# Two transformer blocks on one core: a norm applied as gate-up tiles leave PSUM, Gelu, borders and mixer orders rearranged

## What is computed

```
x = x + post_norm(mixer_2(pre_norm(x)))        # gated delta rule and dilated attention
h = pre_ffn_norm(x)                            # h = x * gain * rstd, rstd per token
u = causal_dwconv(h @ ffn_up, 3 taps) + bias
x = x + post_norm((gelu(gate of u) * val of u) @ ffn_down)
```

## Time and profile before

| | us |
|---|---|
| median of 3 runs | 2065.92 |
| lowest and highest | 2065.55, 2076.42 |
| the profiled execution, its own time | 2066.17 |
| its span, first to last instruction | 2064.3 |
| TensorE busy in it | 1919.4 |
| VectorE, ScalarE, GpSimd busy | 1223.1, 996.8, 652.8 |
| mean granted clock of TensorE | 0.964 |

### The profile page before, as it was taken

The page is one execution under the profiler, slowest core; times in us unless marked ns, Lnnn a source line. Parts: engine busy times, 40 slices in busy tenths (PEclk is TensorE's granted clock), DMA queues, the critical chain, the costliest instruction groups (busy, mean ns, idle before and its releaser), DMA issues.

```text
span 2064.3 us, 41181 instructions
## 1 busy us (share of the span) xinstructions
PE 1919.4 (93%) x15758; PEld 1870.1 (91%) x15758; DVE 1223.1 (59%) x1478; ACT 996.8 (48%) x1304; POOL 652.8 (32%) x595
## 2 busy tenths in 40 slices
PE   6999999999999999999999989879999889779997
PEld 6999999999989999999999989769889789679897
DVE  4655586666456456866664674446664664356655
ACT  5434456544444345564444563445544564445543
POOL 4751301276137513012662016122330025032220
PEclk9999999999999999999999899989999799889999
DMA  6646444465455464444555422114445222124444
GB/s 221 209 164 210 154 144 145 162 206 193 164 195 201 157 215 164 144 146 159 206 190 168 154 102 100 42 64 144 175 144 199 90 102 87 37 82 163 166 164 159
DMA packets 49222, 314.39 MB, mean 152 GB/s; under 512 B 5713, under 2 KB 6865, under 8 KB 19921
## 3 DMA queue, kind: packets, MB, share of 16 engines
q1 hardware_dynamic: 48960, 311.09, 43.7%
q10 hardware_dynamic: 144, 1.69, 0.2%
HBM read 311.71 MB, written 1.05 MB: 152 GB/s over the span
## 4 chain that ended last, share of the span: by engine, by line
PE 62%; DVE 10%; issue 9%; ACT 9%; DMA 5%; POOL 2%; ACTq 1%; DVEq 0%; SPq 0%; POOLq 0%
PE ps L541 15%; PE ps L543 15%; PE ps L542 15%; DMA raw<-in_down_dram 4%; ACT w_hi L1109 4%; DVE w_lo L1567 4%; PE ps L858 3%; PE ps L546 3%; PE ps L547 3%; PE ps L548 3%; DVE conv L1886 2%; ACT conv L1160 2%; PE ps L691 1%; PE ps L731 1%; DVE v L2084 1%
## 5 line engine op out<-in xcount | busy, mean ns | idle before, releaser
L1567 DVE TENSOR_TENSOR w_lo<-raw,w_hi 128x2048 fp32r<-128x2048 f32 (+1 forms) x322 | 713.0, 2215 | 423.6 <-ACT w_hi L1109 423.1
L541 PE MATMUL ps<-xn,w_hi 128*128 128x256 f32 x2688 | 768.5, 286 | 59.6 <-DVE w_lo L1567 14.6
L542 PE MATMUL ps<-xn,w_hi 128*128 128x256 f32 x2688 | 755.7, 281 | 0.0
L543 PE MATMUL ps<-xn,w_lo 128*128 128x256 f32 x2688 | 755.5, 281 | 0.0
L1109 ACT ACTIVATE w_hi<-raw 128x2048 fp32r<-128x2048 f32 (+1 forms) x322 | 562.4, 1748 | 126.5 <-DMA raw<-in_down_dram 83.4
L541 PEld LDWEIGHTS ps<-xn,w_hi 128*128 128x128 f32 x2688 | 516.9, 192 | 74.2 <-issue 44.1
L542 PEld LDWEIGHTS ps<-xn,w_hi 128*128 128x128 f32 x2688 | 515.4, 192 | 0.8 <-issue 0.5
L543 PEld LDWEIGHTS ps<-xn,w_lo 128*128 128x128 f32 x2688 | 515.1, 192 | 0.0
L541 PE MATMUL ps<-h,w_hi 128*128 128x256 f32 x1056 | 294.1, 278 | 4.9 <-DVE w_lo L1567 4.8
L542 PE MATMUL ps<-h,w_hi 128*128 128x256 f32 x1056 | 293.2, 278 | 0.0
L543 PE MATMUL ps<-h,w_lo 128*128 128x256 f32 x1056 | 293.2, 278 | 0.0
(11 more groups left out here) (310 smaller groups left out, 2633.2 us busy)
## 6 DMA issues: line engine op xcount, KB each, us to landing
raw<-in_gu_dram SPq DMA_DIRECT2D x132, 1024.0 KB, 4.9
raw<-in_in_dram SPq DMA_DIRECT2D x70, 1024.0 KB, 4.9
raw<-in_down_dram SPq DMA_DIRECT2D x96, 704.0 KB, 4.1
raw<-in_out_dram SPq DMA_DIRECT2D x16, 1024.0 KB, 4.8
raw<-in_pb_dram SPq DMA_DIRECT2D x4, 1024.0 KB, 4.8
raw<-in_pa_dram SPq DMA_DIRECT2D x4, 1024.0 KB, 4.9
tables_all<-in_tables_dram ACTq DMA_DIRECT2D x1, 1648.0 KB, 7.2
rows<-in_rows_dram SPq DMA_DIRECT2D x2, 768.0 KB, 5.5
```

The costliest lines, as they stand in the source:

```text
L541: pe.matmul(out, w, xh, start=first, stop=False)
L542: pe.matmul(out, w, xl, start=False, stop=False)
L543: return pe.matmul(out, wl, xh, start=False, stop=last)
L1567: dve.tensor_tensor(w_lo[:, r, 0:elems], raw[:, k % RAW_RING, 0:elems], w_hi[:, r, 0:elems], ALU.subtract).then_inc(lo.sem, 1)
```

## The change

1. **Second gate-up.** VectorE multiplies each tile by rstd into conv_in as it leaves PSUM, which frees the pair; all taps read conv_in. ScalarE's order is taps, w_hi of the slot three ahead, Gelu. `v`, its copy and the two forms of low part ahead of the stage go: ScalarE writes xn = x * gain, VectorE its low part, and the sum of squares is made behind the first tile.
2. **Borders.** `rounds` runs body first, then the split; `open_rounds` makes the split of the third slot ahead of the root (ScalarE) or behind the reciprocal (VectorE; in the second block ahead of it). `tile_rounds` takes the place of `rounds` in the down stages. The dummy slots at the end go.
3. **PSUM squares.** ScalarE squares output and down tiles of the second block straight from PSUM and scales them into hm with the gain; TensorE sums the squares chunk by chunk within the stage (`chunk_square`). VectorE takes five chunks of the post norm, GpSimd three.
4. **Mixer orders.** See the lines below. The final norm of the first block goes from VectorE to two wide GpSimd products.
5. **x by another queue.** ScalarE's queue loads x, gains1, ones_d and eps; slot 0 of the weights is split ahead of x.
6. In the first block's output stage the low part of a chunk is written one tile later, and the split comes first.

```diff
-            for c in range(KC):
-                dve.scalar_tensor_tensor(v[:, c], x[:, c], gains2[:, 4 * layer + 2, c:c + 1], rstd[:, 0:T],
-                                         ALU.mult, ALU.mult).then_inc(v_ok.sem, 1)
-                if c >= 2 and c % 2 == 0:
-                    low_even(at, 0, c - 2)
...
             for c in range(KC):
                 x_ready(act, at, 0, c)
+                split_x(c, gains2[:, 4 * layer + 2, c:c + 1])
                 act.activation(sq8[:, c], x[:, c], ACT.Square).then_inc(squared.sem, 1)
...
-                whole = st.name == "gu"
-                if not whole:
-                    for f in range(2):
-                        tile_done(dve, at, st, j, f, g)
-                        dve.tensor_tensor(conv_in[:, j % 2, f], ps[:, 2 * (j % 2) + f, 0:T], rstd[:, 0:T], ALU.mult)\
-                           .then_inc((conv_src, drained)[f].sem, 1)
+                for f in range(2):
+                    tile_done(dve, at, st, j, f, g)
+                    dve.tensor_tensor(conv_in[:, j % 2, f], ps[:, 2 * (j % 2) + f, 0:T], rstd[:, 0:T], ALU.mult)\
+                       .then_inc((conv_src, drained)[f].sem, 1)
...
-                        src = ps[:, 2 * (j % 2) + f, 0:T - s] if whole else conv_in[:, j % 2, f, 0:T - s]
+                        src = conv_in[:, j % 2, f, 0:T - s]
...
+    def rounds(eng, at, st, nxt, count, split, body, behind=None):
         def step(j, g):
             body(j, g)
+            split(at, st.slot0 + j + 1 + LEAD, g, st.elems)
+            if behind:
+                behind(j, g)
...
+    def tile_rounds(eng, at, st, nxt, split, body, steps=cycle):
+        def step(j, g):
+            split(at, st.slot0 + 2 * j + 1 + LEAD, g, st.elems)
+            split(at, st.slot0 + 2 * j + 2 + LEAD, g, st.elems)
+            body(j, g)
+        split(at, st.slot0 + LEAD, 0, st.elems)
+        steps(eng, KC - 2, 2, step)
...
+        def square_out(at, gain, c, src, sq):
+            act.activation(sq[:, c], src, ACT.Square).then_inc(squared.sem, 1)
+            act.activation(hm[:, c], src, ACT.Copy, scale=gains2[:, 4 * at[1] + gain, c:c + 1]).then_inc(x_new.sem, 1)
...
+        def chunk_square(at, n, c, src):
+            pe.wait_ge(squared.sem, squared.upto(at, KC * n + c + 1))
+            ins = pe.matmul(ps[:, AUX, 0:T], ones_d[:], src[:, c], start=c == 0, stop=c == KC - 1)
...
                     if k == 5:
-                        decay_rows_of(1)
+                        query_column()
+                        turn_k()
...
+                if k == 0:
+                    small_product(at, 2 * DN_H, ba_split, ba_hi, ba_lo, SC + 1)
                 if k == 1:
                     rstd_columns(at)
-                    small_product(at, 2 * DN_H, ba_split, ba_hi, ba_lo)
                 if k == 4:
                     decay_rows_of(0)
-                    query_column()
                 if k == 5:
-                    turn_k()
+                    decay_rows_of(1)
...
                 if k == 7:
-                    attend_pv(at, 0, tok[:, V], SC)
                     level_u(LEVELS - 1)
-                    attend_scores(at, 1, 4, SC)
+                    short_scores(at, 2)
+                    short_scores(at, 3)
...
+            attend_out(at, 1, SC)
+            short_turn(at, 3)
+            short_pv(at, 2, tok[:, V])
+            short_pv(at, 3, tok[:, V])
+            head_sums()
+            attend_out(at, 0, SC + 1)
...
+            out_part(0, 0, WC)
+            out_part(1, 0, WC)
+            out_part(2, 0, WC)
+            pe.wait_ge(o_rooted.sem, o_rooted.upto(at, 2))
+            for j in range(3):
+                out_part(j, WC, KC)
+                if j:
+                    chunk_square(at, 0, 2 * j - 2, sq_out)
+                    chunk_square(at, 0, 2 * j - 1, sq_out)
+            out_part(3, 0, KC)
```

More of the change, by code:

```diff
@@ L127 @@
 GROUP = NH // 2
+POOL_ADDS = (1, 4, 7)
+DVE_ADDS = (0, 2, 3, 5, 6)
 RAW_AT = 16 * 1024 + 128
@@ L525, in _ @@
             stream(at, st2["down"], io["down3"])
-        for k in range(LEAD):
-            load((2, DEPTH), k, 0, SLOT, io["in2"][0, k])
         for c in range(KC):
@@ L651, in tile @@
                     last.then_inc(used.sem, 1)
+                    if behind_tile and j and not half:
+                        behind_tile(j - 1)
+            if behind_tile:
+                for j in range(st.pairs):
+                    tile(j, 0)
+                behind_tile(st.pairs - 1)
+                return
             tile(0, 0)
@@ new lines, in _ @@
+            for j in range(3):
[4 more added lines that the diff above has]
+            out_part(3, 0, KC)
+            chunk_square(at, 0, 6, sq_out)
+            chunk_square(at, 0, 7, sq_out)
+            wide(at, st2["gu"], 0, 0, xn, KC, 0, lambda: mean_square_direct(at, 1))
+            wide(at, st2["gu"], 1, 0, xn, KC)
+            with pe.Fori(0, (FC - 2) // 4) as g:
+                for j in range(2, 6):
+                    wide(at, st2["gu"], j, g, xn, KC)
@@ L1496, in _, with short_exp, short_copy @@
                     attend_exp(at, 0)
-                if k == 6:
-                    attend_copy(at, 0, SC)
+            split(at, so.slot0 + 2, 0, SLOT)
             attend_exp(at, 1)
+            act.wait_ge(projected.sem, projected.upto(at, 8))
+            act.activation(four(z_t[:]), four(z_t[:]), ACT.Silu).then_inc(z_ok.sem, 1)
+            act.activation(warm[:, 2:3], eps[:, 0:1], ACT.Exp)
+            def short_exp(u):
+                act.wait_ge(max_ok.sem, max_ok.upto(at, u + 1))
+                for k in range(GROUP):
+                    p = soft[:, 0, k, (u - 2) * P:(u - 1) * P]
+                    act.activation(p, p, ACT.Exp, bias=neg_max[:, u, k:k + 1],
+                                   accum_out=z_sum[:, u, k:k + 1]).then_inc(probs.sem, 1)
+            def short_copy(u):
+                act.wait_ge(pv.sem, pv.upto(at, 2))
+                act.wait_ge(p_turned.sem, p_turned.upto(at, TURNS[u]))
+                copy(p_t[:, u - 2], ps[:, u - 2, :].rearrange("p (k q) -> p k q", k=GROUP)).then_inc(p_out.sem, 1)
             out_copy(1, v_new[:, 0], AUX)
@@ L1838, in _, with low_out @@
             so = st1["out"]
+            def low_out(c):
+                scale_low(at, 1, c, gains1[:, 3 * layer + 2, c:c + 1], xn_lo_odd if c % 2 else xn_lo_even)
             for j in range(4):
+                if j < 3:
+                    split(at, so.slot0 + j + LEAD, 0, SLOT)
                 for f in range(2):
-                    if f == 1 and j < 3:
-                        split(at, so.slot0 + j + LEAD, 0, SLOT)
                     c = 2 * j + f
@@ L2057, in _ @@
[L2057 to L2067 removed]
+            attend_norm(at, 2, 1)
@@ L2091, in post, with add @@
-                scale_next(KC - 2)
-                scale_next(KC - 1)
+                    gain = 4 * layer + 2 if n == 0 else 4 * (layer + 1)
+                    x_ready(dve, at, n, c)
+                    scale_low(at, n, c, gains2[:, gain, c:c + 1], xn_lo_odd if c % 2 else xn_lo_even)
+                follows = k == 1 or layer < DEPTH - 1
+                def add(i):
+                    c = DVE_ADDS[i]
+                    dve.wait_ge(post_dve.sem, post_dve.upto(at, len(DVE_ADDS) * n + i + 1))
+                    dve.tensor_tensor(x[:, c], x[:, c], v[:, c], ALU.add).then_inc(x_dve.sem, 1)
@@ L2094, in _ @@
+                for i, c in enumerate(DVE_ADDS):
+                    dve.tensor_tensor(v[:, c], hm[:, c], rstd[:, 0:T], ALU.mult).then_inc(post_dve.sem, 1)
+                    if i:
+                        add(i - 1)
+                    if follows and i >= 2:
+                        scale_next(i - 2)
+                add(len(DVE_ADDS) - 1)
+                if follows:
+                    for c in range(3, KC):
+                        scale_next(c)
             post(1)
             split(at, so.slot0 + 3 + LEAD, 0, SLOT)
+            open_rounds(at, st2["gu"], split)
```

511 lines of the change are left out of this document (286 added, 225 removed).

## The result

The changed kernel takes 2020.12 us (median of four runs, 2018.53 to 2024.12), against 2065.74 before: 0.977 of the time, 95% interval 0.974 to 0.980. It is faster, by 46 us, where 78 were forecast; 2020 lies above the range, which ended at 2014. The profiled execution took 2018.53 us with a span of 2016.7, so I make the comparison 2064.3 against 2016.7 in spans, 47.6 us.

The account below looks back on a forecast made before the run. TensorE, busy for 93% of the span, was taken as the bound, with time to gain only where it stands or runs at low clock. Terms summed to 78.2 us: 2066.2 to 1988 us, own range 1970 to 2000, full range 1954 to 2014.

Parts of the forecast that it names:

- Gate-up loop: Second block's gate-up: slots fall from 6.06 to 5.6 us (bounds 5.44 and 5.95), 19.2 us gained over two layers.
- The rule that VectorE's taps now contend: Gate-up: taps reading conv_in from SBUF contend with GpSimd; slower rival 8.4 us per slot, 2105 us, chance 0.03.
- Norm ahead of gate-up: Between last output matmul and first gate-up slot's end, norm behind the first tile saves 5.5 us per layer, 11 together.
- Tail: Before the output stage: new mixer orders cut 38.2 us to some 24, 14 per layer; weak-tail rival 2006 us, chance 0.15.
- qkv stage: Second block's qkv: later query column removes waits, 3 us per layer (bounds 0 and 8), plus 1.5 in the first.
- The two new waits that I had named: In qkv: turn_k waits for decay_in(0), and the second decay rows for q2; counted within the 3 us gain per layer.
- two whole-tile GpSimd products at a time when GpSimd is idle: 0: First layer's qkv stage: final scaling of x moves from eight VectorE steps (3.4 us) to GpSimd, at no gain or cost.
- Start: Kernel start: x by another queue and three wide GpSimd sums, first matmul about 12.5 us, 4 us gained (bounds 0 and 7).
- x lands late: Start's lower bound: three MB sharing the engines delay x, so the gain is 0 instead of 4 us.
- Down stages and behind: Second block's down stages and what follows, both layers: PSUM squares and no dummy slots at the end gain 3.5 us together.
- The reciprocal no longer waits for w_lo: Behind the first layer's down stage, where the first matmul waits 12.0 us: this saves 1 to 3 us.
- First block: low_out one tile later gives 6.5 us in output stage and gap behind (bounds 2 and 10), down-stage split order 0.5.

Follow-up runs that it names:

- the one that mends five parts: Changed kernel with the old start, final x and post norms on VectorE, squares behind the last tile, norm ahead of the last split: 2001.93 us.

## Why the prediction failed, and where it held

- **Gate-up loop: right within the stage, with a cost behind it that I left out.** Slots 1 to 21 took 118.7 and 117.5 us where I took 117.6, so 18.9 us came for the 19.2. TensorE's wait for the taps went, as forecast. But the loop of VectorE and ScalarE takes 5.87 us, inside my bounds of 5.44 and 5.95, and TensorE goes faster than that on the slots it has in hand. The sizes came from the qkv stage, where the tap starts after 0.45 us and takes 0.91; here 0.74 and 1.10. What is left over is paid in the second down slot. Of the 22 gate-up stages of the changed kernel and of its edits that leave this loop alone, nine ran at the slow pitch and were followed by a wait of 2.82 to 3.05 us there, thirteen mostly at the fast one, by 4.05 to 4.42: what TensorE gains in the stage it waits for behind it. The rule that VectorE's taps now contend did little harm: one tap of four is held, 1.02 us instead of 0.59, and the four still end with w_hi; w_lo starts first and keeps its 2.29, and GpSimd, which has time, stands.
- **Norm ahead of gate-up: too high.** 3.6 and 2.9 us came for 5.5 each. TensorE starts 7.2 us sooner behind the output stage, but its first slot takes 12.0 and 12.8 us instead of 8.4.
- **Tail: right, mis-sized.** From the same matmul on, 17.4 us in each layer where 14 were taken, and 20.9 left for the estimated 24. The waits for exponents and copies shrank to under 1 us each.
- **qkv stage: wrong in both layers.** "I take 3, twice" failed: from 75.1 and 74.8 us the stretch went to 84.2 and 76.9, a loss of 2.1 us in layer 1, where no GpSimd product stands in it. The two new waits that I had named and thought cheaper than the old ones are its rows: turn_k waits 1.7 us for gam, the second decay rows 2.7 for q. Layer 1 as a whole came out at -16.6 for -17, and that is luck: 5.1 us lost here against 3.4 gained in the tail and 1.3 in the side stage.
- **qkv stage, layer 0: a second step failed**, "two whole-tile GpSimd products at a time when GpSimd is idle: 0". It cost 3.4 to 3.7 us at the same clock; the 6.8 us more at 0.50 in the first profile cost as much again, and in the nine others with this hold the time at 0.50 was anything from 22.2 to 30.7 us. I named the cover on GpSimd's side and did not ask what VectorE does meanwhile, though my own row of 3.79 beside 2.29 was its warning.
- **Start: wrong**, +3.2 for -4. I had counted three wide sums in place of seven as a gain in GpSimd's time, and they hold w_lo and the low parts for 5.3 us; the queue cost 2 us more. The bound "x lands late" was set at 0 gain, where it should have gone below.
- **Down stages and behind: wrong by 16.0 us.** (a) "The reciprocal no longer waits for w_lo": true at the end, where that slot is left out, not in layer 0, where the rows show both copies ahead of it. What is behind the stage went from 12.0 to 12.4 us, where I had -5; taking the squares away from there freed nothing, since the w_lo outlasts them. (b) At the end 16.1 became 13.8, not 11.5: VectorE's products took 0.94, and with all of them on VectorE it is 11.9. (c) In the stream, 5.7 and 8.8 us for the 3.0 of the squares. The rest has three parts. One is the wait in the second down slot, 2.8 and 4.4 us where 2.4 and 1.5 were in all; its w_hi stands behind the last Gelu. The second is the clock, at 0.50 behind that wait, which makes the matmuls there 1.6 and 2.4 us longer. The third is the slow pitch behind the squares, at 4.5 ns a matmul 1.1 and 0.7 us more than before. Together with the 3.0 they make 6.2 and 9.0, slightly too much. I did not look at the last slots of the gate-up stage, where a loop that hides its latency has to pay it.
- **First block:** 12.6 us for the 7. The output stage and the gate-up behind it gave 5.8 for 6.5. The last 3.6 of the rest are one gate-up stage that was slow in the profile of before (127.7) and fast in that of after (124.1), luck and no effect.
- **Range.** The bounds of the terms were added up for the upper end of the gain only; the case that several "nothing" terms cost something at once had no place. The pitch I could have read in the stages of before, 124.2 and 127.7 us for the same work. The three runs of before, whose highest is 10.9 us over the lowest, also said that one execution can move by that much; whether the pitch is all of it is not shown.

## What to carry to other kernels

Work moved to an idle GpSimd is free only if VectorE reads no second SBUF operand meanwhile. If it must be there, cut it into short instructions, or place it so that VectorE's long one starts first. When a loop's latency is hidden inside, price its last iterations too. Read an edit in its own stage before the whole time, since one and the same program spread over 11 us in four executions, and within the stage compare the clock, since half of a difference of 7.2 us was clock here. Begin the stretches before and after at the same instruction: here the tail is 20.9 us from the matmul at which the 38.2 of before begin, and 23.8 from the last side tile.

## What the runs showed of the hardware beyond what I expected

**Two pitches at one granted clock.** With the granted clock at 1.00 and no waits, the same 128x256 matmuls come either 113.3 or 117.8 ns apart. An unbroken stream keeps its pitch from its first few matmuls on; in none of the fourteen profiles does one change it. What breaks it is a wait or other matmuls among them, and behind the break it runs at either. Whole gate-up stages ran at one or the other: 122.8 or 127.2 us. The same program took another pattern of such stages in its second profile, so the code alone does not fix it. But nor is it always open. In the first block's mixers 480 large matmuls are cut into 14 streams by small matmuls alone, without a wait. There fast and slow streams stand in the same order in all fourteen profiles and both layers: of 599 steps from matmul to matmul at most three differ by over 2 ns. So where the breaks repeat to the ns, the pitch repeated too, and it varied where waits make the breaks. Behind an fp32 square in the stream it was the slow one for 78 to 100% of the steps in both second-block down stages of all eleven profiles that have these squares; with the squares behind the stage the share was 38 and 50% in the kernel before, 6 and 0% in the edit that moves them back, and 6 and 100% in the one that mends five parts. What in TensorE sets it stays open.

**The hold lasts one instruction.** w_lo 6.67 us behind a GpSimd product of 4.59, GpSimd's 0.74 stretched to 2.45 by a w_lo of 2.29, VectorE's 0.41 to 0.94 beside products of 0.78: each time the later starter ends its own length after the end of the first.
